# Routing of a mixture of experts: the order of the steps between a norm and the first expert tile

## The reference, cut to what matters

```python
def moe_swiglu(h, w_router, b_router, w1, w3, w2):
    logits = (h @ w_router).astype(jnp.float32) + b_router.astype(jnp.float32)
    top_val, top_idx = lax.top_k(logits, TOP_K)          # 2 of 8 experts for each token
    top_w = jax.nn.softmax(top_val, axis=-1)
    gate = jnp.einsum('blk,blke->ble', top_w, jax.nn.one_hot(top_idx, N_EXPERTS, ...))
    out = jnp.zeros_like(h)
    for e in range(N_EXPERTS):
        out = out + gate[..., e:e + 1] * swiglu(h, w1[e], w3[e], w2[e])
    return out
...
    x = x + gt2 * moe_swiglu(modulate(rmsnorm(x, g_ffn), sh2, sc2), w_router[j], ...)
```

## Time and profile before

| what | value |
|---|---|
| three runs | 2690.32, 2695.33, 2697.02 us |
| median | 2695.33 us |
| the profiled execution, its own time | 2690.35 us |
| its span | 2688.5 us |
| PE busy | 2459.7 us (91%) |
| DVE busy | 1269.5 us (47%) |
| ACT busy | 849.0 us (32%) |
| mean granted TensorE clock | 0.972 of full speed |
| DMA | 648.75 MB, mean 241 GB/s |

### The profile page before, as it was taken

How to read it: one execution, slowest core, us unless ns; L and a number is a source line. 1 busy time by engine, 2 the same in 40 slices (tenths; PEclk the granted TensorE clock), 3 DMA queues, 4 the chain that set the end, 5 groups by cost and what they waited for, 6 DMA issues and landing times.

```text
span 2688.5 us, 39100 instructions
## 1 busy us (share of the span) xinstructions
PE 2459.7 (91%) x15923; PEld 1670.1 (62%) x15923; DVE 1269.5 (47%) x1936; ACT 849.0 (32%) x1212; POOL 217.9 (8%) x247
## 2 busy tenths in 40 slices
PE   7997999998787888879998998998989998898998
PEld 2864769955322322326776776777857996664996
DVE  3306645523300101004665665657455777895664
ACT  2101544411000000003553554554423544102553
POOL 0401200001000000000000000000000007362000
PEclk9998999999999999999998998999999999999999
DMA  8727175577899999998765765756556655534452
GB/s 295 173 78 266 25 259 177 185 270 279 329 411 412 410 416 407 411 413 320 262 240 176 262 223 189 261 210 218 189 217 211 215 186 181 195 126 133 157 182 85
DMA packets 248153, 648.75 MB, mean 241 GB/s; under 512 B 12623, under 2 KB 102896, under 8 KB 225656
## 3 DMA queue, kind: packets, MB, share of 16 engines
q10 hardware_dynamic: 111760, 358.68, 35.3%
q1 hardware_dynamic: 130648, 275.51, 29.2%
q0 software_dynamic: 5584, 12.28, 2.4%
HBM read 645.38 MB, written 1.05 MB: 240 GB/s over the span
## 4 chain that ended last, share of the span: by engine, by line
PE 74%; DMA 15%; DVE 6%; issue 2%; ACT 1%; POOL 1%; ACTq 1%; SPq 0%; POOLq 0%; DVEq 0%
DMA ring<-in_moe_w 14%; PE bank L1518 6%; PE bank L695 5%; PE bank L1536 5%; PE bank L1537 5%; PE bank L1535 5%; PE bank L697 4%; PE bank L696 4%; PE bank L1545 4%; PE bank L1546 4%; PE bank L1547 4%; PE bank L710 3%; PE bank L628 2%; PE bank L1579 2%; PE bank L662 2%; PE bank L1967 2%
## 5 line engine op out<-in xcount | busy, mean ns | idle before, releaser
L1057 DVE TENSOR_TENSOR w_low<-ring,w_high 128x1024 fp32r<-128x1024 f32 x252 | 305.6, 1225 | 128.5 <-ACT w_high L861 126.2
L628 PE MATMUL bank<-ring,arena 128*64 128x512 f32 (+1 forms) x1280 | 268.6, 549 | 73.5 <-DMA ring<-in_moe_w 73.5
L861 ACT ACTIVATE w_high<-ring 128x1024 fp32r<-128x1024 f32 x252 | 265.8, 1060 | 195.8 <-PE bank L697 194.2
L2442 DVE TENSOR_TENSOR ring_low<-ring,up_high 128x1024 fp32r<-128x1024 f32 x186 | 227.1, 1279 | 113.3 <-ACT up_high L2084 112.9
L1535 PE MATMUL bank<-ht_low,up_high 128*128 128x256 f32 x960 | 272.9, 284 | 0.0
L628 PEld LDWEIGHTS bank<-ring,arena 128*64 128x64 f32 x1280 | 81.5, 136 | 256.6 <-DMA ring<-in_moe_w 157.2
L2084 ACT ACTIVATE up_high<-ring 128x1024 fp32r<-128x1024 f32 x186 | 182.7, 1047 | 84.3 <-PE bank L1547 73.0
L1041 DVE TENSOR_TENSOR HT<-HT,bank 128x512 f32<-128x512 f32 (+1 forms) x20 | 12.4, 622 | 378.6 <-PE bank L628 378.6
L1536 PE MATMUL bank<-ht_high_cf_up,up_high 128*128 128x256 f32 x640 | 183.0, 286 | 0.0
L1535 PEld LDWEIGHTS bank<-ht_low,up_high 128*128 128x128 f32 x960 | 180.3, 188 | 1.6 <-DVE arena L2318 0.8
L1537 PE MATMUL bank<-ht_high_cf_up,ring_low 128*128 128x256 f32 x640 | 181.1, 283 | 0.0
(11 more groups left out here) (419 smaller groups left out, 4221.2 us busy)
## 6 DMA issues: line engine op xcount, KB each, us to landing
ring<-in_moe_w ACTq DMA_DIRECT2D x340, 1024.0 KB, 14.7
ring<-in_w_ada SPq DMA_DIRECT2D x48, 1024.0 KB, 6.9
ring<-in_ada_w SPq DMA_DIRECT2D x48, 1024.0 KB, 4.9
ring<-in_ffn_w_up SPq DMA_DIRECT2D x44, 1024.0 KB, 5.0
ring<-in_ffn_w SPq DMA_DIRECT2D x33, 1024.0 KB, 5.1
ring<-in_ret_w_in SPq DMA_DIRECT2D x24, 1024.0 KB, 5.2
ring<-in_ffn_w_down SPq DMA_DIRECT2D x22, 1024.0 KB, 4.9
ring<-in_w_in SPq DMA_DIRECT2D x12, 1024.0 KB, 10.3
```

The source lines that it names most:

```text
L628: mm = pe.matmul(PS[b][64 * n:64 * n + 64, 0:cols], XGF[:, ks * h + k, :], w[:, k, cols * n:cols * n + cols], start=h + k == 0, stop=ks * ...
L861: act.activation(WH[half % SPLIT][:, :], slot(moe_first + i)[:, HALF * (half % 2):HALF * (half % 2) + HALF], ACT.Copy)\
L1057: dve.tensor_tensor(out=WL[half % SPLIT][:, :], in0=slot(i)[:, HALF * (half % 2):HALF * (half % 2) + HALF], in1=WH[half % SPLIT][:, :], op ...
L2442: dve.tensor_tensor(out=low_of(base + tile, q), in0=slot(base + tile)[:, HALF * q:HALF * q + HALF], in1=high_of(part, n), op=ALU.subtract) ...
```

## The change

It reorders the steps between the mixer and the first expert tile, and changes the form of one product.

- The eight transposes of half t = 0 stand behind tile 3 of `ada2_0`, those of t = 1 behind tiles 4 and 5, and tiles 6 and 7 come behind the router product.
- The router product has WR stationary (8 columns) and HT moving (256 columns): 8 matmuls instead of 16. Its result, 8 x 256, is copied to SBUF by ScalarE (`LOGITS`) and transposed by two small matmuls. VectorE starts behind those (`route_counted` 2).
- VectorE fills VALID, KIND0, the ends of GATE_R and SLOT_R and EXPV before the router's result is there; IOTAN, IOTAX, the memset of PGT and the copies GTN, GTX come later than before, the last three behind the first `pick`.
- The rounds are worked out directly behind the gates. SLOT follows `small_i`. PM of the first round is made as soon as SLOT_R is there (`route_ready` 5), and `gather` waits for that; the gates come afterwards (`pick_ready`).
- `mod_ready(2, 0)` and `mod_ready(2, 1)` stand behind all that on VectorE.
- The first four expert tiles wait each for its own slot (tile i-7), not for the whole list.

```diff
         def moe_tensor(pe, mod_rows):
             pe.wait_ge(sem("route_landed"), 64)
+            for k in range(KD):
+                mm = pe.matmul(PS[0][0:E8, 0:SEQ], WR[:, k, :], HT[:, k, :], start=k == 0, stop=k == KD - 1)
+            mm.then_inc(sem("route_counted"), 1)
+            pe.wait_ge(sem("pair_exp"), 1)
             for t in range(TT):
-                for k in range(KD):
-                    mm = pe.matmul(PS[0][:, 8 * t:8 * t + 8], HT[:, k, P * t:P * t + P], WR[:, k, :], start=k == 0, stop=k == KD - 1)
+                mm = pe.transpose(PS[0][:, SEQ + 8 * t:SEQ + 8 * t + 8], LOGITS[:, P * t:P * t + P], ident[0:E8, 0:E8])
             mm.then_inc(sem("route_counted"), 1)
+            mod_rows(sa, 2, 0, 6, KD, 4)
...
             mod_rows(sa, 2, 1, 0, KD, 5)
-            pe.wait_ge(sem("modr_ready"), 7)
...
+            pe.wait_ge(sem("route_ready"), 5)
+            gather()
             pe.wait_ge(sem("pick_ready"), 1)
-            gather()
             turn_gates()
...
         def moe_scalar(act, ch):
+            act.wait_ge(sem("route_counted"), 1)
+            ch.step(act.activation(LOGITS, PS[0][0:E8, 0:SEQ], ACT.Copy), sem("pair_exp"))
...
-            sa.wait_done(act, moe_first - 1)
             for i in range(AHEAD):
+                sa.wait_done(act, moe_first + i - RING)
                 moe_load(act, first, i)
...
         def moe_vector(dve, ch, mod_ready):
-            dve.wait_ge(sem("route_counted"), 1)
             dve.wait_ge(sem("route_landed"), 64)
+            dve.memset(VALID, 1.0)
+            dve.memset(KIND0, 0.0)
+            dve.memset(GATE_R[:, :, COLS:NEXT], 0.0)
+            dve.memset(SLOT_R[:, :, COLS:NEXT], -1.0)
+            for i in range(2):
+                link(dve.tensor_copy(EXPV[:, E8 * i:E8 * i + E8], IOTA[:, 0:E8]))
+            dve.wait_ge(sem("route_counted"), 2)
...
-            link(dve.memset(VALID, 1.0))
-            link(dve.memset(KIND0, 0.0))
-            link(dve.memset(PGT, 0.0))
...
-            for i in range(2):
-                link(dve.tensor_copy(EXPV[:, E8 * i:E8 * i + E8], IOTA[:, 0:E8]))
-                link(dve.tensor_copy(IOTAN[:, NARROW * i:NARROW * i + NARROW], IOTA[:, 0:NARROW]))
...
-                link(dve.tensor_copy(GTN[h, :], ada_part(5)[h, BANK * i:BANK * i + BANK]))
-            for i in range(4):
-                link(dve.tensor_scalar(IOTAX[:, EXTRA * i:EXTRA * i + EXTRA], IOTA[:, 0:EXTRA], float(WIDE), None, ALU.add))
...
-                link(dve.tensor_copy(GTX[h, :], ada_part(5)[h, SEQ * i:SEQ * i + SEQ]))
-            dve.wait_ge(sem("route_counted"), 2)
-            for t in range(TT):
-                link(dve.scalar_tensor_tensor(out=SLOT[:, t, :], in0=PS[1][:, 8 * t:8 * t + 8], scalar=1.0, in1=MASK[:, t, :],
-                                              op0=ALU.add, op1=ALU.mult))
+            dve.wait_ge(sem("route_counted"), 3)
             count = PS[1][:, 16:24]
...
             for t in range(TT):
+                link(dve.scalar_tensor_tensor(out=SLOT[:, t, :], in0=PS[1][:, 8 * t:8 * t + 8], scalar=1.0, in1=MASK[:, t, :],
+                                              op0=ALU.add, op1=ALU.mult))
+            for t in range(TT):
                 link(dve.tensor_copy(BYV[:, 0:E8], SLOT[:, t, :]))
...
+                link(dve.tensor_copy(CUR[:, t:t + 1], SLOT_R[:, t, 0:1]))
+            for t in range(TT):
+                ins = dve.tensor_scalar(PM[:, t, :], IOTA, CUR[:, t:t + 1], None, ALU.is_equal)
+            link(ins, sem("route_ready"))
+            for t in range(TT):
                 for i in range(2):
                     link(dve.tensor_copy(BYV[:, E8 * i:E8 * i + E8], GATE[:, t, :]))
                 by_round(GATE_R[:, t, 0:COLS], BYV)
+            for i in range(2):
+                link(dve.tensor_copy(IOTAN[:, NARROW * i:NARROW * i + NARROW], IOTA[:, 0:NARROW]))
+            for i in range(4):
+                link(dve.tensor_scalar(IOTAX[:, EXTRA * i:EXTRA * i + EXTRA], IOTA[:, 0:EXTRA], float(WIDE), None, ALU.add))
...
-            pick(link, slice(0, 1))
+            pick(link, slice(0, 1), True)
+            link(dve.memset(PGT, 0.0))
...
+                link(dve.tensor_copy(GTN[h, :], ada_part(5)[h, BANK * i:BANK * i + BANK]))
...
+                link(dve.tensor_copy(GTX[h, :], ada_part(5)[h, SEQ * i:SEQ * i + SEQ]))
+            mod_ready(sa, 2, 0, 4)
             mod_ready(sa, 2, 1, 5)
...
-            rows_behind(sa, 2, 0, 2)
-            turn("moe")
+            rows_behind(sa, 2, 0, 2, 0, 4)
+            turn("moe", 0, lambda t: rows_behind(sa, 2, 0, 2, 4, 6) if t else None)
             turned("moe")
             moe_tensor(pe, mod_rows)
```

More of the change, by code:

```diff
@@ L1000, in pick @@
                     dve.tensor_scalar(PGN[:, t, :], IOTAN, where, gate, ALU.is_equal, ALU.mult)
[L1001 to L1002 removed]
+                    ins = dve.tensor_scalar(PGX[:, t, :], IOTAX, where, gate, ALU.is_equal, ALU.mult)
+                    if not first:
+                        ins = dve.tensor_scalar(PM[:, t, :], IOTA, where, None, ALU.is_equal)
                 ins.then_inc(sem("pick_ready"), 1)
```

25 lines of the change are left out of this document (12 added, 13 removed).

## The result

| | before | changed |
|---|---|---|
| median of 8 runs | 2693.14 us | 2678.38 us |
| lowest and highest | 2690.17 to 2697.02 | 2675.01 to 2687.41 |
| ratio, 95% interval | | 0.995 [0.994, 0.996] |
| profiled execution, its span | 2690.35, 2688.5 | 2679.57, 2677.8 |

A forecast was written before the change was run, and what follows sets the result against it. DMA bounds the narrow rounds, so the expert stream's start decides. Tile 4 issued 12.0 us earlier plus 0.5 gives 12.5: 2677.9 from the profiled 2690.35, 2682.8 from the median 2695.33, taken as 2683; range 2677 to 2690.

The forecast's parts named there:

- Transposes: Moved transposes ahead of the router product: HT ready at 657.2, but the last table lands at 658.8, so 3.2 us won.
- Router product: Product 5.2 us, with copy and small transposes 6.4 to VectorE's start; costs 0.5 us, between -1.0 and +2.8.
- VectorE's chain: From VectorE's start to PM 13.5 us against 23.1 before, so `gather` could start at 678.8.
- Ahead of `gather`: PE's last modulation tile is late, landing at 679.2 with 1.0 us for sharing; `gather` starts at 680.6, 10.6 us earlier.
- `gather`: PE comes to it without a pause, so it takes 3.84 instead of 5.21 us: 1.4 us more gained.
- The stream's start: Expert tile 4 issued 12.0 us earlier, at 687.1, queued before DMA runs dry: up to 1.3 us more, 0.5 taken.
- What is late next: After `gather`, VectorE ends at 688.7 and PE's first expert tile starts at 692.3; price nothing if the stream has no hole.
- rival B: PE's late start ahead of L614 at 1.2 GHz decides; stream hole 3 to 8 us, gain 4.5 to 9.5, 2688; chance 0.13.
- the signs of being wrong: `gather` released by VectorE later than 682, a DMA hole between 685 and 705, or a longer narrow or wide stage.
- Rival A: Router's result as late as before, product 7.4 us at 1.2 GHz; `gather` about 682, gain 9.5, time 2686; chance 0.14.
- Rival C: Stream gains more than `gather`: no hole, no collision, VectorE's 678.8 decides; gain 15 us, time 2680; chance 0.08.
- Rival D: Low clock stays through the first narrow tiles, 3.9 us each instead of 1.94; PE bounds, slower at 2704; chance 0.03.

The follow-up runs named there:

- v_early_dma: `v_early` with the four routing tables also loaded ahead of the mixer's last products, to another place in SBUF; 2676.06 us, ratio 0.995.
- v_defer_dma: `v_defer` with the four routing tables also loaded ahead of the mixer's last products; 2673.92 us, ratio 0.994.
- a_oldproduct: Changed kernel with the router product in its old form (HT stationary, no copy, no small transposes); 2683.40 us, ratio 0.997.
- a_waitall: Changed kernel with the first four expert tiles waiting for the whole list again; 2679.23 us, ratio 0.995.
- v_early: Changed kernel with IOTAN, IOTAX, PGT, GTN and GTX filled while VectorE waits for the router's result; 2677.53 us, ratio 0.995.
- v_defer: `v_early` with the last of the eight modulation tiles of `ada2_1` multiplied behind `gather` instead of ahead of it; 2675.43 us, ratio 0.994.
- b_turns: Kernel before with only the places of the transposes changed; 2690.66 us, ratio 0.999.
- a_midtables: Changed kernel with PGT, GTN, GTX, IOTAN and IOTAX filled between the gates and the counts again; 2679.76 us, ratio 0.996.

## Why the prediction was right, point by point

The time was in the range, in the right direction, and 4.6 us below the forecast. Most terms held, one price failed, and one that was charged was not there. (Of the slices it read, 407 to 416 GB/s stand in 12 to 18, counted from 1, not 407 to 418 in 11 to 18; nothing rests on it.) From the zero of each trace:

1. *Transposes.* Forecast: product at 11.5 us, released by the last table. It started at 12.0 behind 3.62 us of waiting for `in_t_before`. `v_early_dma` and `v_defer_dma` confirm it from the other side: with the tables there, it starts at 9.3.
2. *Router product.* Forecast 6.4 us to VectorE's start; 6.15 (658.09 to 664.24, clock 0.72). The product took 3.61 us at the high clock in `v_defer_dma`, as the mixer's row had said; which of the two it gets could not be read from the trace of before, and the bound of 7.4 was not needed. `a_oldproduct` shows that at the lower clock the change of form gave and took nothing.
3. *VectorE's chain.* Forecast 13.5 us from its start to PM; 664.24 to 677.7 is 13.5.
4. *Ahead of `gather`.* Forecast 33.3 with the last modulation tile late, not VectorE; measured 32.87 with that tile as releaser of the product ahead of it. It landed at 31.4 (forecast 31.9, of which 1.0 was for sharing with the expert tiles). That 1.0 us was not there: the tile landed 2.47 us behind the one ahead of it, as without a second queue (2.44 in `a_waitall`), and only 0.16 MB of expert tiles had moved before its last packet. The tile ahead of it landed at 28.9 instead of 28.4, which hides half of this. With the rule of the Trainium skill (DMA: Bandwidth & Descriptors, Queues, rings and completion order) that a DMA engine goes round between its queues the trace of `v_early` agrees so far that packets of both queues moved in the same 3 us. But the last packets of the modulation tile came 0.39 us apart instead of 0.31, not twice as far apart as the prediction had taken, and the price was at most 0.6 us.
5. *`gather`.* Forecast 3.8 us; 3.82 at clock 1.00.
6. *The stream's start.* Tile 4 was issued at 39.4 (forecast 39.8). I had the four first tiles through 41.5 us from the zero, and they were at 43.5, since I had given the modulation tile's share no time of its own. In the pair that the forecast went by, tile 4 lands 11.4 us earlier, 1.1 less than the forecast sum; that the mean of both pairs is 12.5 comes from the kernel before, which is later in its second profile.
7. *What is late next.* **This is the step that failed**: "Price: nothing if the stream has no hole". VectorE's end was right (687.93 less 646.07 is 41.9; forecast 41.4). But the matmuls of L619 behind 3.51 us of idle ran at the low clock for most of their time, 6.25 us instead of 3.60, PE's first tile came at 48.0 instead of 45.0, and tile 7 was issued at 50.2 instead of 47.1. I had this clock in rival B and left it out of the sum, though `gather` had shown the same thing before in the earlier trace rows. The windows of the changed kernel: the product (step 2), the end of VectorE's chain (3), `gather` (5), and what follows:

```profile
658.09:664.24 6.15, 5.68 (x22) 2.08 (x26) 0.41 (x6) 0.80 (x2) 0.00 (x0) 0.72 1.01 423
...
673.60:677.72 4.12, 3.25 (x33) 0.81 (x28) 3.58 (x17) 0.00 (x0) 0.00 (x0) 1.00 0.91 339
...
678.90:682.80 3.90, 3.86 (x34) 3.66 (x33) 3.47 (x17) 0.01 (x1) 0.00 (x0) 1.00 1.05 399
...
686.30:693.10 6.80, 5.17 (x6) 2.19 (x7) 2.80 (x5) 0.00 (x0) 0.00 (x0) 0.50 1.03 396
693.10:697.00 3.90, 3.90 (x31) 2.14 (x31) 2.78 (x5) 0.00 (x0) 0.00 (x0) 1.00 0.54 216
697.00:703.00 6.00, 6.00 (x50) 3.42 (x48) 0.72 (x2) 1.67 (x2) 0.00 (x0) 1.00 0.94 305
703.00:1226.00 523.00, 434.89 (x2089) 149.52 (x2085) 48.43 (x124) 32.52 (x63) 0.00 (x0) 1.00 1.02 411
```

The clock is 0.50 from 686.3 to 693.1, and right behind it the DMA share is 0.54: the hole, which the prediction had named among the signs of being wrong. The landing of tile 7 comes 4.74 us behind tile 6 (4.00 in the second profile). Tiles 4 to 8 take 12.6 and 13.1 us, before 11.2 and 10.8; that is the 1.9 us that are lost between tile 4 and tile 8. `v_defer`, where PE's wait is 0.18 us and the matmuls take 3.70, has no hole (10.2 us). No run keeps the wait of 3.51 us at the high clock, so that the clock alone made the hole is worked out, not shown: without the 2.65 us tile 7 would have been issued at 47.5, 3.6 us before tile 6 landed. Another 0.8 us go until tile 209 in single late landings (tile 15 comes 3.78 us behind tile 14), for which I found no cause. The local forecast of 12.5 us was 3.1 too much.

Rival A would have had `gather` at about 34.7 and the modulation group at 26.0; the group's first tile stood at 22.6, so it is out. Rival B was right in kind and held for one hole of 2.2 us, below its 3 to 8, with tile 7 issued at 50.2 where it had 50.7. Rival C is what `v_defer` is: with no hole, and with VectorE and not the tile ahead of `gather`, it gains 13.2 us against the mean of the two profiles before; the changed kernel did not do it. Rival D is out: the last of the windows above shows clock 1.00 over the narrow rounds, and 411 GB/s as before.

The median came out lower than 2683 although the local gain was smaller. Of the 14.8 us between the medians the stage of the change has 9.4; the last stage is 3 to 6 us shorter in the changed kernel's profiles, and nothing in my working spoke of that. That the number came so close is luck in this respect: a local gain 3.1 us too small and a later stage that no term named make up for each other. (The kernel before also had a median 2.2 us lower in these runs than in the three that I went by.)

## What to carry to other kernels

Where a stream that fills DMA bounds a stage, two things ahead of it set its start: when its first queued tile is issued, and when the consumer uses its first tile. Follow both, since the ring turns a late consumer into a hole a few tiles later. When a wait is shortened, look at what PE does behind the next wait: matmuls behind a few us of idle took up to 1.8 times as long here, and one part of a change can then seem worthless when it is undone alone. And a DMA's time from issue to landing holds what its own queue still had to do: before a second queue is blamed for it, compare it with a run in which the second queue was empty.

## What the runs showed of the hardware

- The same instructions behind an idle stretch of PE: `gather` 3.82 to 3.84 us at clock 1.00, 6.34 in `b_turns`, 6.49 in `v_early`, and in the second profile of the kernel before:

```profile
691.82 6.78 PE L597 MATMUL bank<-arena,H 128*128 128x128 f32 x32 [8.57 <-DVE arena L1002]
```

  The profile from which the prediction was made had caught it at 5.21, so the price of the low clock there was larger than I could read. The low clock can also come without a fresh wait of PE just ahead: in `v_early` the wait of 2.02 us stands before the matmuls ahead of `gather`.
- The same modulation tile of 1 MB landed 4.7 us after its issue in the kernel before, where the tile ahead of it landed 0.5 us behind that issue, and 7.3 to 7.7 us after it where SP's queue held more and no expert tile was on the way (`a_midtables`, `b_turns`, `a_waitall`). A second busy queue stretched its last packets of 8 KB from 0.31 to 0.39 us each (`b_turns`, `v_early`).
- Identical work behind the change took 866 to 872 us in the last stage. A few us gained or lost there are no evidence on the change.
